# Expert loop: token rows gathered in quarters and turned by VectorE in mid-slot, in place of TensorE transposes at the slot's end

## The reference: what is computed

```python
logits = jnp.einsum('nd,de->ne', xf, P['router'][m], preferred_element_type=jnp.float32)
probs = jax.nn.softmax(logits, axis=-1)
top_p, top_i = lax.top_k(probs, TOP_K)          # TOP_K = 2
top_p = top_p / jnp.sum(top_p, axis=-1, keepdims=True)
...
for e in range(N_EXPERTS):                       # 8 experts, D_FF_EXPERT = 1408
    y = y + gates[:, e:e + 1] * _swiglu(xf, moe_w_gate[m, e], moe_w_up[m, e], moe_w_down[m, e])
```

## Time and profile before

| | us |
|---|---|
| median of 3 runs | 1988.81 (1988.74 to 1989.03) |
| profiled execution, its own time | 1989.05 |
| its span | 1987.4 |
| TensorE busy | 1971.7 (99%) |
| VectorE busy | 1519.9 (76%) |
| ScalarE busy | 1132.2 (57%) |
| GpSimd busy | 264.6 (13%) |
| splits of weights, VectorE L2122 | 643.0 in 306 instructions |
| splits of weights, ScalarE L1416 | 541.4 in 306 instructions |

### The profile page before, as it was taken

One profiled execution on the slowest core, in us unless ns is written; L12 is line 12 of the kernel. 1 busy time (PEld: TensorE's weight loads), 2 busy tenths in 40 slices (PEclk: granted clock), 3 DMA queues, 4 the chain that ended last, 5 costly groups with the idle time before them and its releaser, 6 DMA issues. The chain is left out here.

```text
span 1987.4 us, 31304 instructions
## 1 busy us (share of the span) xinstructions
PE 1971.7 (99%) x11754; PEld 1762.5 (89%) x11754; DVE 1519.9 (76%) x1692; ACT 1132.2 (57%) x1378; POOL 264.6 (13%) x284
## 2 busy tenths in 40 slices
PE   9999999999999999999999999999999999999998
PEld 5898689999999999989878988888888888888886
DVE  5548678877767774765863498989999989989997
ACT  5227664322212223532865478788777888887775
POOL 1230100000000000132000046001111111010113
PEclk9999999999999999999999999999999999999999
DMA  9220433344454443422004589999999999999998
GB/s 343 97 84 6 148 119 127 128 139 154 142 161 138 159 135 89 124 79 76 1 1 49 220 345 385 405 393 397 390 396 388 405 386 397 386 401 395 401 389 251
DMA packets 155246, 458.64 MB, mean 231 GB/s; under 512 B 15713, under 2 KB 87633, under 8 KB 137457
## 3 DMA queue, kind: packets, MB, share of 16 engines
q1 hardware_dynamic: 131488, 379.42, 51.3%
q0 software_dynamic: 21792, 75.65, 10.9%
q10 hardware_dynamic: 1872, 2.26, 0.3%
HBM read 440.72 MB, written 17.69 MB: 231 GB/s over the span
## 5 line engine op out<-in xcount | busy, mean ns | idle before, releaser
L2122 DVE TENSOR_TENSOR w_lo<-mraw,w_hi 128x1792 fp32r<-128x1792 f32 (+2 forms) x306 | 643.0, 2114 | 80.7 <-ACT w_hi L1416 79.4
L1416 ACT ACTIVATE w_hi<-mraw 128x1792 fp32r<-128x1792 f32 (+2 forms) x306 | 541.4, 1775 | 166.7 <-PE ps L2828 162.2
L2826 PE MATMUL ps<-w_hi,xs_lo 128*128 128x448 f32 (+1 forms) x816 | 309.7, 380 | 1.0 <-DVE xs_lo L2127 0.8
L2828 PE MATMUL ps<-w_hi,xs_hi 128*128 128x448 f32 (+1 forms) x816 | 305.0, 374 | 0.0
L2827 PE MATMUL ps<-w_lo,xs_hi 128*128 128x448 f32 (+1 forms) x816 | 304.6, 373 | 0.0
L1519 DVE TENSOR_TENSOR sub_lo<-zone,sub_hi 128x1024 fp32r<-128x1024 f32 (+2 forms) x112 | 129.5, 1158 | 116.9 <-ACT sub_hi L1066 116.5
L1066 ACT ACTIVATE sub_hi<-zone 128x1024 fp32r<-128x1024 f32 (+2 forms) x112 | 109.2, 977 | 176.7 <-PE ps L2409 93.7
L2826 PEld LDWEIGHTS ps<-w_hi,xs_lo 128*128 128x128 f32 x816 | 153.3, 188 | 25.1 <-DVE w_lo L2122 7.4
L2828 PEld LDWEIGHTS ps<-w_hi,xs_hi 128*128 128x128 f32 x816 | 153.3, 188 | 19.2
L2827 PEld LDWEIGHTS ps<-w_lo,xs_hi 128*128 128x128 f32 x816 | 153.4, 188 | 17.9
L2394 PE MATMUL ps<-f_hi,sub_lo 128*128 128x320 f32 x704 | 162.2, 312 | 0.0
(11 more groups left out here) (371 smaller groups left out, 3655.1 us busy)
## 6 DMA issues: line engine op xcount, KB each, us to landing
mraw<-in_moe_pieces SPq DMA_DIRECT2D x136, 1024.0 KB, 8.0
mraw<-in_moe_pieces SPq DMA_DIRECT2D x136, 896.0 KB, 7.8
in_cos<-in_w_mods POOLq DMA_DIRECT2D x72, 512.0 KB, 3.7
mraw<-in_moe_pieces SPq DMA_DIRECT2D x34, 768.0 KB, 8.1
zone<-in_w_in SPq DMA_DIRECT2D x13, 1024.0 KB, 5.2
zone<-in_w_ada SPq DMA_DIRECT2D x12, 1024.0 KB, 9.8
zone<-in_w_gate SPq DMA_DIRECT2D x11, 1024.0 KB, 5.1
zone<-in_w_up SPq DMA_DIRECT2D x11, 1024.0 KB, 5.0
```

The source lines that it names most:

```text
L1416: nc.scalar.activation(w_hi[:, n % SPLITS, a], mraw[:, n % MRING, a], ACT.Copy).then_inc(w_hi_ready, 1)
L2122: nc.vector.tensor_tensor(w_lo[:, n % SPLITS, a], mraw[:, n % MRING, a], w_hi[:, n % SPLITS, a].bitcast(f32), ALU.subtract).then_inc(w_spl ...
L2826: nc.tensor.matmul(out, a_lo, b_hi, start=start, stop=False)
L2828: return nc.tensor.matmul(out, a_hi, b_hi, start=False, stop=stop)
```

## The change

The rows of the next slot come in quarters. `token_of` now holds, in partition 32q + t, the row numbers of quarter q (256 features) of tokens t, 32 + t, 64 + t and 96 + t; four small DMAs fetch it. Four indirect DMAs gather quarter rows of 1 KB, 128 in each. VectorE's 32x32 block transpose (`nc.vector.transpose`, one instruction over 32 blocks, in place) then puts feature 8p + k of every token into partition p: its blocks take every eighth element, so it reads and writes with a step of 32 bytes, and the result is read by the two splits with the same step (`x_turned_at`). The features of a k-block are thus p, 8 apart, and the gate and up weights are laid out to match on the host, as are the one-hot matmuls of slot 0 (`htok_chunks`). The eight TensorE transposes of a slot and their waits go. ScalarE and VectorE make `xs_hi` and `xs_lo` in mid-slot, ahead of `turned(2)`, where they did it behind.

```diff
-        token_of, slot_info = sb("token_of", [P, 16], i32), sb("slot_info", [P, 16], i32)
+        token_of, slot_info = sb("token_of", [P, 4, 16], i32), sb("slot_info", [P, 16], i32)
...
+        htok_chunks = htok.rearrange("p t (c k) -> p t k c", k=KC)
...
+        x_rows = xs.rearrange("p (g n) -> p g n", g=4)
+        x_turned_at = xs.rearrange("p (g t k) -> p k g t", g=4, k=KC)
+        x_blocks = xs.rearrange("p (g t k) -> p g k t", g=4, k=KC)
...
-        G_EACT, G_ETR = len(CHUNKS), 5
+        G_EACT, G_ETR = len(CHUNKS), 3
         TR_OF = {0: 0, 1: 1, 2: 2, "xa": 3, "xb": 4}
+        SPLIT_NTH = {0: 1, 1: 2, "xa": 3, "xb": 4, 2: 5}
+        def split_nth(c, last):
+            return SPLIT_NTH[c] - 2 * (last and c == 2)
...
-                pool.dma_start(token_of[:], slot_tokens[at, 0:16]).then_inc(tokens_in, 16)
+                for q in range(4):
+                    pool.dma_start(token_of[32 * q:32 * q + 32], slot_tokens[at, 16 * (1 + q):16 * (2 + q)].rearrange("(g t) n -> t g n", g=4)).then_inc(tokens_in, 16)
+            quarter_rows = token_rows.rearrange("t (q n) -> (t q) n", q=4)
             def slot_x():
-                pool.indirect_dma_start(out=xs, out_offset=None, in_=token_rows,
-                                        in_offset=bass.IndirectOffsetOnAxis(ap=token_of[:, 0:1], axis=0)).then_inc(xs_in, 16)
+                for g in range(4):
+                    pool.indirect_dma_start(out=x_rows[:, g], out_offset=None, in_=quarter_rows,
+                                            in_offset=bass.IndirectOffsetOnAxis(ap=token_of[:, g, 0:1], axis=0)).then_inc(xs_in, 16)
...
-                pool.wait_ge(xs_in, 16 * (s + 1))
+                pool.wait_ge(xs_in, 64 * (s + 1))
                 slot_tokens_in(bass.ds((s + 2) * P, P))
                 pool.wait_ge(y_evac, s + 2)
                 pool.dma_start(yslots[bass.ds(s * P, P), :], ybuf).then_inc(y_stored, 16)
                 slot_info_in(s + 1)
-                pool.wait_ge(etr_done, 2 + G_ETR + 5 * s + TR_OF["xb"] + 1)
-                pool.wait_ge(tokens_in, 16 * (s + 2))
+                pool.wait_ge(etr_evac, 2 + 5 * s + SPLIT_NTH["xb"])
+                pool.wait_ge(tokens_in, 64 * (s + 2))
...
+                def x_hi(half):
+                    act.wait_ge(x_turned, s + 1)
+                    act.wait_ge(pc_done, pieces_done(s, EPIECE_AT["up", 2, 4]))
+                    a = slice(4 * half, 4 * half + 4)
+                    nc.scalar.activation(xs_hi[:, a, :].rearrange("p k (g t) -> p k g t", g=4), x_turned_at[:, a], ACT.Copy).then_inc(ehi_ready, 1)
                 def turned(c):
-                    j = TR_OF[c]
-                    if c in ("xa", "xb"):
-                        half = ("xa", "xb").index(c)
-                        dst, kn = xs_hi[:, 4 * half:4 * half + 4, :], 4
-                    else:
-                        dst, kn = ea_hi[:, BLK[c][0]:BLK[c][1], :], BLK[c][1] - BLK[c][0]
-                        act.wait_ge(pc_done, pieces_done(s, -1))
-                    tr_hi(dst, turn_bank(c), 2 + G_ETR + 5 * s + j + 1, kn)
+                    act.wait_ge(pc_done, pieces_done(s, -1))
+                    tr_hi(ea_hi[:, BLK[c][0]:BLK[c][1], :], turn_bank(c), 2 + G_ETR + 3 * s + c + 1, BLK[c][1] - BLK[c][0])
...
-                ahead(13, 14, 15, 16)
+                ahead(13, 14)
+                if not last:
+                    x_hi(0)
+                ahead(15)
+                if not last:
+                    x_hi(1)
+                ahead(16)
                 turned(2)
-                ahead(17)
-                if last:
-                    return
-                turned("xa")
-                ahead(18, 19)
-                turned("xb")
-                ahead(20)
+                ahead(17, 18, 19, 20)
...
-                    nc.vector.tensor_tensor(htok[:, 0, 0:512], htok[:, 0, 0:512], shift_for[0][:, 0:512], ALU.add).then_inc(first_row_half, 1)
-                    nc.vector.tensor_tensor(htok[:, 0, 512:1024], htok[:, 0, 512:1024], shift_for[0][:, 512:1024], ALU.add).then_inc(htok_ready, 1)
+                    first, shift = htok_chunks[:, 0], shift_for[0].rearrange("p (c k) -> p k c", k=KC)
+                    nc.vector.tensor_tensor(first[:, 0:4], first[:, 0:4], shift[:, 0:4], ALU.add).then_inc(first_row_half, 1)
+                    nc.vector.tensor_tensor(first[:, 4:8], first[:, 4:8], shift[:, 4:8], ALU.add).then_inc(htok_ready, 1)
...
+                def turn_x():
+                    dve.wait_ge(xs_in, 64 * (s + 1))
+                    nc.vector.transpose(x_blocks, x_blocks).then_inc(x_turned, 1)
+                def x_lo(half):
+                    a = slice(4 * half, 4 * half + 4)
+                    dve.wait_ge(ehi_ready, 2 + 5 * s + SPLIT_NTH[("xa", "xb")[half]])
+                    nc.vector.tensor_tensor(xs_lo[:, a, :].rearrange("p k (g t) -> p k g t", g=4), x_turned_at[:, a],
+                                            xs_hi[:, a, :].bitcast(f32).rearrange("p k (g t) -> p k g t", g=4), ALU.subtract).then_inc(etr_evac, 1)
                 def turned(c):
-                    j = TR_OF[c]
-                    if c in ("xa", "xb"):
-                        half = ("xa", "xb").index(c)
-                        a = slice(4 * half, 4 * half + 4)
-                        dst, hi, kn = xs_lo[:, a, :], xs_hi[:, a, :], 4
-                    else:
-                        a = slice(*BLK[c])
-                        dst, hi, kn = ea_lo[:, a, :], ea_hi[:, a, :], BLK[c][1] - BLK[c][0]
-                    tr_lo(dst, hi, turn_bank(c), 2 + 5 * s + j + 1, kn)
+                    a = slice(*BLK[c])
+                    tr_lo(ea_lo[:, a, :], ea_hi[:, a, :], turn_bank(c), 2 + 5 * s + split_nth(c, last), BLK[c][1] - BLK[c][0])
                 def product(c):
                     o, w = 512 * bank_of(c, 1), CHUNKS[c][1] - CHUNKS[c][0]
                     dve.wait_ge(pc_done, pieces_done(s, EPIECE_AT["up", c, 4]))
                     dve.wait_ge(esilu_ready, 3 * s + c + 1)
-                    dve.wait_ge(etr_done, 2 + 5 * s + TR_OF[2] + 1)
+                    dve.wait_ge(etr_done, 2 + 3 * s + TR_OF[2] + 1)
...
+                if not last:
+                    turn_x()
                 ahead(13)
                 product(2)
-                ahead(14, 15, 16)
+                ahead(14)
+                if not last:
+                    x_lo(0)
+                ahead(15)
+                if not last:
+                    x_lo(1)
+                ahead(16)
                 turned(2)
-                ahead(17)
+                ahead(17, 18, 19)
                 if last:
                     return
-                turned("xa")
-                ahead(18, 19)
-                turned("xb")
...
-                                               htok[:, t, (4 * half + k) * P:(4 * half + k + 1) * P], onehot[:, t, :],
+                                               htok_chunks[:, t, 4 * half + k], onehot[:, t, :],
...
-                    if c == "xa":
-                        pe.wait_ge(xs_in, 16 * (s + 1))
-                    if c in ("xa", "xb"):
-                        x_transposes(("xa", "xb").index(c)).then_inc(etr_done, 1)
-                        return
...
-                use(14)
-                if not last:
-                    tr("xa")
-                use(15, 16)
-                if not last:
-                    tr("xb")
-                use(17)
+                use(14, 15, 16, 17)
...
-    out["token_i"] = np.where(np.arange(P) == 2, token % P * 2 + token // N_LAT, token).astype(np.int32)
+    at = np.arange(P)
+    quarter = np.where((at >= 16) & (at < 80), at // 16 - 1, -1)
+    line = np.where(at == 2, token % P * 2 + token // N_LAT, token)
+    out["token_i"] = np.where(quarter >= 0, 4 * token + quarter, line).astype(np.int32)
     out["zero_row"] = np.zeros((1, D_MODEL), np.float32)
-    out["no_tokens"] = np.where(np.arange(P) == 2, np.arange(SLOTS * P)[:, None] % P * 2, 0).astype(np.int32)
+    out["no_tokens"] = np.where(at == 2, np.arange(SLOTS * P)[:, None] % P * 2, np.maximum(quarter, 0)).astype(np.int32)
...
-        w = x["moe_w_" + u].reshape(NE, -1, P, x["moe_w_" + u].shape[-1])[:, k0:k1, :, c0:c1]
-        return w.transpose(0, 2, 1, 3).reshape(NE, P, -1)
+        w = x["moe_w_" + u][0]
+        if u == "down":
+            w = w.reshape(NE, FCE, P, D_MODEL)
+        else:
+            w = w.reshape(NE, P, KC, D_FFE).transpose(0, 2, 1, 3)
+        return w[:, k0:k1, :, c0:c1].transpose(0, 2, 1, 3).reshape(NE, P, -1)
     a = {n: x[n] for n in _WEIGHTS}
     a["moe_pieces"] = np.concatenate([expert_piece(*p) for p in EPIECES], axis=2)
```

More of the change, by code:

```diff
@@ L668, in build @@
         y_gated, x_copied, slot_gate_ready = sem("y_gated"), sem("x_copied"), sem("slot_gate_ready")
+        x_turned = sem("x_turned")
         hot_ready, hot_turned, hot_out, row_at_ready = (sem(n) for n in ("hot_ready", "hot_turned", "hot_out", "row_at_ready"))
@@ L970, in _ @@
             slot_info_in(0)
```

(14 more changed lines are left out.)

## The result

The changed kernel takes 2030.28 us (median of four runs, 2028.8 to 2031.06) against 1988.78 (1988.74 to 1989.03): a ratio of 1.0207, 95% interval 1.0194 to 1.022. The profiled execution is the fastest of the four (2028.8); its span is 2027.2 us where before's is 1987.4, so 39.8 us are to be found.

What follows compares the result with a forecast made beforehand. The prediction took TensorE to bound the loop, with VectorE at 90% close behind. +21 us from 16 slots and +19 from the start, +40 on 1988.81, gave 2029 us, range 1999 to 2056.

Steps and rivals of the forecast that it cites:

- TensorE's transposes, 0.46 a group: Expert loop: removing two groups of four TensorE transposes saves 0.46 us a group, 0.92 a slot, 14.7 over 16 slots.
- VectorE's transpose, 2.2 us: Mid-slot on VectorE: the added stepped transpose of 128x1024 takes 2.2 us, bounds 1.26 and 2.43.
- The x parts, 0.97 from start to start: Mid-slot on VectorE: each x part, one of three operands stepped, takes 0.97 us instead of 0.60; bounds 0.60 and 1.2.
- The spare of 1.8 us: Ahead of piece 16: VectorE has 1.8 us spare before TensorE stalls; the stall beyond it is 2.2 us a slot.
- ScalarE's copies at nothing: Two x copies moved to mid-slot, 0.58 us each, perhaps 1.2 stepped, cost nothing as long as VectorE is later.
- The steady wait at nothing: Slots 2 to 15: VectorE's new mid-slot wait for the four gathers costs nothing, with 3.2 us of spare.
- Waits of 4.2 and 15.0 us in slots 0 and 1: VectorE waits for late gathered rows, 4.2 us in slot 0 and 15.0 in slot 1, adding 19.2 us.
- The stepped matmuls, "swallowed: 0": Ahead of the loop: 80 stepped gathering matmuls cost up to their 9.38 us again, swallowed by slots 0 and 1's waits: 0.
- Sum: Whole kernel: +21 us from the slots and +19 from the start make +40 us, 2029 us.
- A: Rival: stepped access is free on VectorE, transpose 1.26 us and x part 0.60; 2004 us; chance 0.17.
- B: Rival: gathered rows come late in every slot, VectorE waiting 1.8 us in 14 slots; 2064 us; chance 0.13.
- C: Rival: faster, if stepped access is free and slot 2's rows land before about 1240; 1984 to 1989 us; chance 0.06.

Runs made afterwards that it cites:

- e9: Changed kernel with adjacent slot-0 matmuls, slot 2's rows requested before hot rows, x gathers before y store, early half transposes into PSUM, x parts at slot's end: 1980.84 us.
- e1: Changed kernel with every stepped access of the change made adjacent, order, gathers and waits kept (features no longer match the weights): 2004.27 us, ratio 1.0077.
- e6: Changed kernel with e5's start; VectorE turns x in two halves, read stepped, written unstepped into PSUM, the second behind the last activation part: 1997.02 us.
- e3: Changed kernel with only slot 0's one-hot matmuls and first shift additions on adjacent columns (slot 0's features don't match the weights): 2033.09 us, ratio 1.0222.
- e2: Changed kernel with only the VectorE transpose's blocks made of adjacent words; x parts and slot 0's matmuls stay stepped (features don't match the weights): 2014.34 us.
- e4: Changed kernel with the two x parts and ScalarE's copies moved back behind the last ea part; transpose stays mid-slot, everything stepped stays: 2016.65 us, ratio 1.0137.
- e7: As e6, but each half is turned in place, so x parts and ScalarE's copies read with step 32 bytes: 2014.47 us, ratio 1.0122.
- e5: Changed kernel with slot 0's token rows as unstepped moving side, x gathers before the y store, slot 2's rows before most hot rows; loop work unchanged: 2021.17 us.

## Why the prediction was right, and where its terms were not

The forecast was 2029 us (1999 to 2056) and slower; measured 2030.28. The mechanism in the loop was right, with one size too low. At the start the term was too high and its mechanism was not the one forecast. The two errors cancel, so the closeness of the number is luck. That the kernel is slower, and inside the range, is not: the 27 us of the loop alone give 2016.

- **TensorE's transposes, 0.46 a group.** Nearly right: in e9, where TensorE waits for nothing in the steady slots, a slot is 0.83 us shorter than before, 0.42 a group; forecast 0.92.
- **VectorE's transpose, 2.2 us.** Right: 2.21. The row of 20 stepped elements was the nearer one, and the bound at the full rate is what e1 has (1.235, forecast 1.26).
- **The x parts, 0.97 from start to start.** Too low: 1.11 (1.18 long). One stepped operand of three brought it near the upper bound of 1.2; the middle was no guide.
- **The spare of 1.8 us.** Right. With the measured durations the prediction's own sum gives 2.10 + 2 x 1.11 - 1.8 = 2.5, less 0.92 is +1.6 a slot (+1.7 with the 0.83 of e9); measured +1.69. In e1 it gives 1.15 + 2 x 0.60 - 1.8 - 0.92 = -0.4, measured -0.27. But the stall isn't all at piece 16: by the starts of the pieces in TensorE's rows (slots 3 to 13) 0.6 us of it come at pieces 13 and 14, and 1.9 at 16.
- **ScalarE's copies at nothing.** They take 1.18 us where they took 0.58 (in the bounds). In the changed kernel VectorE is the later one. In e6, ScalarE's second copy stands in a tight place, with its 1.6 us of waiting a slot ahead of the copy of piece 19.
- **The steady wait at nothing.** Right. In slot 2 the first gather starts 11.9 us behind the y product (forecast 12.0) and the rows are in at 28.0 (forecast 26.0, bounds to 27.2), where VectorE comes at 29.5: a spare of 1.4 us, not 3.2. Slot 14 has 1.3. In the other eleven of slots 2 to 14 the rows are in at 22.8 to 25.4, and the spare is 4.0 to 6.7. The gathers took 1.93 us each instead of 1.84.
- **Waits of 4.2 and 15.0 us in slots 0 and 1.** Failed as stated: 0 and 0.8. The text said that I would be wrong if the idle time in slot 1 were under 8 us, and for this step I was. It had GpSimd's second round of token DMAs at 1228.0; it came at 1220.76, since the first had landed sooner. And VectorE wanted the rows at 1248.0, not at 1239.8, since the loop had begun later.
- **The stepped matmuls, "swallowed: 0".** They took 19.32 us instead of 9.38, "as much again", and were not swallowed: 8.9 us of it arrive at the first expert matmul and 0.9 at piece 1 of slot 0. The step of the prediction that failed is that "the waits of slots 0 and 1 end by GpSimd's clock" whatever the start of the loop. GpSimd's clock moved with it: the token DMAs landed in 1.9 us instead of the 4.4 to 5.6 of e3, and from its first gather on GpSimd ran 10 to 14 us ahead of e3.
- **Sum.** Start 19.2 forecast, 12.7 measured: 1.7 in the first 42 us, which the change doesn't explain, 9.2 up to the first expert matmul, 1.0 more in slot 0 (0.9 of it at piece 1) and 0.8 of waiting. The slots 21 forecast, 27 measured (16 x 1.69). The two errors, of about 6 us each, cancel.

The rivals: A is refuted by the transpose's 2.21 us; e1 is A's kernel, and its time is A's (2004). The Trainium skill, VectorE: DVE Perf Modes, section Mode 1× (REGULAR), which would have made the change rival A, doesn't hold here for steps of 32 bytes. The figures of the Trainium skill, Vector Engine (DVE) Microarchitecture Reference, section 5.2 (Measured stream behaviour on trn2), fit in size: 1.98 ns a column where all operands hop and 2.50 in its rows with short steps; the trace has 2.21 us for 1024, some 2.0 ns each beyond the fixed part. For one source that hops it gives 1.73, and the x parts took somewhat more, some 2.0 ns (1.18 us for 512). B (rows late in every slot) was 1.3 us away in the two closest slots and 4.0 or more in the others. C needed slot 2's rows by about 1240 and VectorE had them at 1248.8; in e9 they are there when VectorE wants them, at 1233.4, and that kernel is faster, with the loop mended as well.

Open: the delay of 1.65 to 2.30 us in the first 42 us of every changed kernel, and why an x part with the same step takes 1185 ns in the changed kernel, 1145 in e2, 1152 in e4 and 1129 in e7. The adjacent transpose isn't the reason, since e4 and e7 have none. No run tests either.

## What to carry to other kernels

Count access with a step of 32 bytes nearly double (1.7 to 1.8 times on VectorE here) before moving work to an engine, and put the step into one instruction (here the transpose's source, with its result in PSUM), so that all later readers have adjacent words. For work that moves to an engine at 90%, the place counts for more than the share: add up that engine's chain from its last idle point to the hand-over that the bounding engine takes; here what fitted in front was free and the rest was paid in full. Where two delays meet (a late start, late rows), don't take one of them as a fixed clock. Taking the larger alone gave 19.2 here, and 11.0 were measured beside the delay of the first 42 us: ask which DMAs and queues the first delay speeds up, and try the kernel without it before it is called free.

## What the runs showed of the hardware

- Step of 32 bytes, 4-byte elements. VectorE: 32x32 block transpose of 128x1024, 1.235 us adjacent, 2.21 with both sides stepped; 128x512 with the source alone stepped and PSUM written, 1.15 to 1.17 us, against 1.22 with both stepped in place (e7). A subtraction of 128x512 with one of three operands stepped: 0.686 us adjacent, 1.13 to 1.18 stepped. ScalarE's copy of 128x512: 0.61 and 1.18.
- TensorE: a float32 matmul with 128 moving columns whose stationary side is stepped. The loads of that side fill the 19.3 us that the 80 matmuls take:

```profile
L2833 PEld LDWEIGHTS ps<-rb,zone 128*128 128x128 f32 x79 | 18.9, 335 | 0.5 <-ACT ps L1413 0.5
```

  With adjacent columns (e3) the same load takes 192 ns, and 80 matmuls 9.38 us.
- With the same rows as the moving side, read without a step, 20 matmuls of 512 columns took 9.10 us (e5). The eight transposes behind them read with a step of 32 bytes and took 1.16 us; their loads took 194 ns each, those of the adjacent transposes just before 144.
- A token DMA of 8 KB landed in 1.9 us while the DMA engines moved 9 GB/s, and in 4.4 to 5.6 beside the weight stream (e3).
